# Side operations and stage joins moved by one contraction tile, and weight splits cut, in a two-layer attention and recurrence kernel

## The reference

```python
u = causal_depthwise_conv(cv_a * sigmoid(cv_b), conv_w, conv_b)
u = silu(layernorm(u, conv_ln_g, conv_ln_b))
y_conv = (u @ w_conv_pw) * silu(cv_gate)
x = x + concatenate([y_conv, y_fox, y_mem]) @ w_out
...
q = rms(q, q_g); k = rms(k, k_g)
att = softmax(q @ k.T * scale + bias) @ v * silu(a_z)
hg = rms(hgrn2(g_q, g_f, g_i), o_g) * silu(g_z)
x = x + gate * (concatenate([att, hg]) @ w_out_2)
```

## Time and profile before

| what | value |
|---|---|
| median of 3 runs | 1893.55 us (1892.36 to 1894.06) |
| the profiled execution, its own time | 1892.65 us |
| its span, first to last instruction | 1890.9 us |
| PE busy | 1877.2 us, 99% |
| DVE, ACT, POOL busy | 62%, 42%, 10% |
| chain that ended last | PE 94%, DVE 3%, ACT 2% |

### The profile page before, as it was taken

One profiled execution on the slowest core, in us unless ns is written; L12 is line 12 of the kernel. 1 busy time (PEld: TensorE's weight loads), 2 busy tenths in 40 slices (PEclk: granted clock), 3 DMA queues, 4 the chain that ended last, 5 costly groups with the idle time before them and its releaser, 6 DMA issues.

```text
span 1890.9 us, 25550 instructions
## 1 busy us (share of the span) xinstructions
PE 1877.2 (99%) x8756; PEld 1546.3 (82%) x8756; DVE 1174.7 (62%) x1708; ACT 789.0 (42%) x1155; POOL 187.7 (10%) x193
## 2 busy tenths in 40 slices
PE   9999999999999999999999999999999999999999
PEld 8888888888888877887788888888888888887887
DVE  6665568888888877777745444445555555556332
ACT  6543333333333373224544444444545454554111
POOL 3500000000000002442000000000112121210000
PEclk9999999999999999999999999999999999999999
DMA  7344144544444426775122222221222122123441
GB/s 280 111 156 178 67 158 176 177 177 168 162 164 172 156 89 221 235 244 197 70 92 90 71 88 92 92 92 67 90 82 73 67 89 89 67 89 129 146 147 67
DMA packets 50407, 244.70 MB, mean 129 GB/s; under 512 B 5688, under 2 KB 6968, under 8 KB 29760
## 3 DMA queue, kind: packets, MB, share of 16 engines
q1 hardware_dynamic: 49920, 241.02, 36.0%
q10 hardware_dynamic: 448, 3.17, 0.4%
HBM read 235.75 MB, written 8.41 MB: 129 GB/s over the span
## 4 chain that ended last, share of the span: by engine, by line
PE 94%; DVE 3%; ACT 2%; issue 0%; DVEq 0%; ACTq 0%; another core or an unknown queue 0%
PE ps_p L599 27%; PE ps_p L601 26%; PE ps_p L600 26%; PE ps_s L919 1%; PE ps_o L751 1%; PE ps_t L735 1%; DVE w_lo L1451 1%; PE ps_x L618 1%; DVE act_lo L2012 0%; ACT act_hi L1239 0%; PE ps_s L724 0%; PE ps_s L723 0%; PE ps_s L725 0%; ACT w_hi L1006 0%; PE ps_o L624 0%
## 5 line engine op out<-in xcount | busy, mean ns | idle before, releaser
L599 PE MATMUL ps_p<-act_hi,w_hi 128*128 128x512 f32 x2272 | 910.6, 401 | 3.5 <-DVE act_lo L1855 1.7
L601 PE MATMUL ps_p<-act_hi,w_lo 128*128 128x512 f32 x2272 | 886.7, 390 | 0.0
L600 PE MATMUL ps_p<-act_lo,w_hi 128*128 128x512 f32 x2272 | 885.9, 390 | 0.0
L601 PEld LDWEIGHTS ps_p<-act_hi,w_lo 128*128 128x128 f32 x2272 | 426.5, 188 | 91.6
L599 PEld LDWEIGHTS ps_p<-act_hi,w_hi 128*128 128x128 f32 x2272 | 427.2, 188 | 88.2 <-issue 3.3
L600 PEld LDWEIGHTS ps_p<-act_lo,w_hi 128*128 128x128 f32 x2272 | 427.5, 188 | 80.8 <-issue 1.4
L1006 ACT ACTIVATE w_hi<-raw 128x2048 fp32r<-128x2048 f32 x154 | 294.5, 1912 | 413.7 <-PE ps_p L601 395.2
L1451 DVE TENSOR_TENSOR w_lo<-raw,w_hi 128x2048 fp32r<-128x2048 f32 x153 | 350.8, 2293 | 91.5 <-ACT w_hi L1006 80.1
L1728 DVE CUSTOM_DVE_ANT_0 mkv<-mkv,c_all 128x1024 f32<-128x1024 f32 x96 | 145.0, 1546 | 4.4 <-DVE wk L1493 2.9
L2200 POOL TENSOR_TENSOR hz<-hqk,hd 128x128 f32<-128x128 f32 x56 | 38.8, 693 | 743.7 <-DVEq L2070 692.7
L2187 POOL TENSOR_TENSOR ssq_a<-ssq_a,wk 128x512 f32<-128x512 f32 x15 | 36.3, 2420 | 733.4 <-ACT wk L1259 733.4
(11 more groups left out here) (318 smaller groups left out, 1879.6 us busy)
## 6 DMA issues: line engine op xcount, KB each, us to landing
raw<-wt_dram SPq DMA_DIRECT2D x156, 1024.0 KB, 4.8
mkv<-ada_dram SPq DMA_DIRECT2D x96, 512.0 KB, 4.4
qkv<-xT_dram SPq DMA_DIRECT2D x16, 256.0 KB, 2.8
spill_dram<-Y SPq DMA_DIRECT2D x16, 256.0 KB, 2.2
hqk<-spill_dram SPq DMA_DIRECT2D x16, 256.0 KB, 2.7
out_dram<-wk SPq DMA_DIRECT2D x16, 256.0 KB, 2.0
Y<-xT_dram SPq DMA_DIRECT2D x3, 1024.0 KB, 10.1
mem_raw<-memT_dram SPq DMA_DIRECT2D x4, 512.0 KB, 10.6
```

The costliest lines, as they stand in the source:

```text
L599: mm(o, wh, hi[:, k, 0:n], start=at == 0, stop=False)
L600: mm(o, wh, lo[:, k, 0:n], start=False, stop=False)
L601: last = mm(o, wl, hi[:, k, 0:n], start=False, stop=at == KT - 1)
```

## The change

It moves work on PE, ACT, DVE and SP, and cuts a few instructions in two. No matmul is added or removed.

- Each channel is squared once it is centred. `conv_z(0)` goes ahead of the sum of the squares. PE's two sums go to places 10 and 6.
- `act_hi` and `act_lo` 4 to 7 are rewritten ahead of `ln_silu((2, 3))`. After `pointwise` the low parts lag the multiplications by one tile.
- In the first head of att the query's square goes between the quarters of the third weight tile, the key's square ahead of the fourth weight tile, which is split in halves. PE's sums go to places 2 and 7.
- In hg `chunk_states` goes from place 9 to 10, and `out_sum` from 2 to 3.
- In the last head DVE makes the low parts of tiles 0 and 1 ahead of the turned pairs, and the second weight tile of out2 is split in halves, on the first of which PE starts.
- The last tile's addition and store are cut in halves.

Only the declarations of four semaphores are left out here, beside unchanged lines:

```diff
@@ -567,13 +571,18 @@
                     sp.wait_ge(s_out, 2 * i + j + 1)
+                    if isinstance(i, int) and i + j == 8:
+                        sp.dma_start(out[15][:, 0:S // 2], wk[:, j, 0:S // 2]).then_inc(s_store[j], 16)
+                        sp.wait_ge(s_out, 17)
+                        sp.dma_start(out[15][:, S // 2:S], wk[:, j, S // 2:S]).then_inc(s_store[j], 16)
+                        continue
                     sp.dma_start(out[2 * i + j], wk[:, j, :]).then_inc(s_store[j], 16)
...
             for j in range(2):
-                sp.wait_ge(s_store[j], 16 * 16)
+                sp.wait_ge(s_store[j], 16 * (16 + j))
@@ -581,10 +590,12 @@
             def project(phase, i, j, hi=act_hi, lo=act_lo, n=S, order=range(KT), hooks=None, use=None, used=None,
-                        quartered=False):
+                        quartered=False, halved=False):
                 s = slot(phase, j)
-                if not quartered:
+                if halved:
+                    pe.wait_ge(out_half, 1)
+                elif not quartered:
                     pe.wait_ge(w_split, tile_no(phase, i, j) + 2)
@@ -592,6 +603,8 @@
                         pe.wait_ge(third_split, at // 4 + 1)
+                    elif halved and at == KT // 2:
+                        pe.wait_ge(w_split, tile_no(phase, i, j) + 2)
                     elif use == "y2":
@@ -816,8 +829,8 @@
                 return lambda: side("gate", 0, k, body)
-            project("gate", 0, 0, hooks={9: channel_sum(0)})
-            project("gate", 0, 1, hooks={5: channel_sum(1)})
+            project("gate", 0, 0, hooks={10: channel_sum(0)})
+            project("gate", 0, 1, hooks={6: channel_sum(1)})
             project("gate", 0, 2)
@@ -885,7 +898,7 @@
                     first_pair()
-                    sums, scored = {3: lambda: square_sum(0), 8: lambda: square_sum(1)}, (14, 15)
+                    sums, scored = {2: lambda: square_sum(0), 7: lambda: square_sum(1)}, (14, 15)
                 else:
@@ -970,12 +983,12 @@
-                project("hg", i, 0, hooks=None if isinstance(i, int) and i == 0 else {2: out_sum})
+                project("hg", i, 0, hooks=None if isinstance(i, int) and i == 0 else {3: out_sum})
                 project("hg", i, 1, hooks={15: lambda: side("hg", i, 0, turn_keys)})
...
                                            8: lambda: turn_value("hg", i, 1, hvT[:, :], QT),
-                                           9: chunk_states, 11: turn_pairs, 13: within, 15: across},
+                                           10: chunk_states, 11: turn_pairs, 13: within, 15: across},
                         used=h_used if isinstance(i, int) and i == 7 else None)
@@ -985,7 +998,7 @@
                 project("out2", i, 0, use="y2", hooks={3: last_sum} if first else None)
-                project("out2", i, 1)
+                project("out2", i, 1, halved=first)
             loop(pe, "out2", out2, head=1)
@@ -1212,8 +1225,8 @@
             split("gate", 0, 0)
-            act.wait_ge(ln_ready.sem, ln_ready.at("gate", 0, 1))
             for c in range(NCONV):
+                act.wait_ge(channel_centred, c + 1)
                 fn(qkv[:, c, :], Y[:, c, :], ACT.Square).then_inc(ln_squares, 1)
@@ -1228,20 +1241,24 @@
             split("gate", 0, 2)
-            act.wait_ge(ln_ready.sem, ln_ready.at("gate", 0, 2))
+            act.wait_ge(ln_ready.sem, ln_ready.at("gate", 0, 1))
             ln_silu((0, 1))
...
             split("gate", 0, 3)
-            ln_silu((2, 3))
...
+            def y_hi_used(order_):
+                for k in order_:
+                    act.wait_ge(x_used, k + 1) if k < KT - 1 else act.wait_ge(proj_done, tile_no("out1", 0, 0) + 1)
+                    y_hi([k])
+
             act.wait_ge(heads_done.sem, heads_done.at("fox", 7, 1))
-            for k in range(4, KT):
-                act.wait_ge(x_used, k + 1) if k < KT - 1 else act.wait_ge(proj_done, tile_no("out1", 0, 0) + 1)
-                y_hi([k])
+            y_hi_used(range(4, 8))
+            ln_silu((2, 3))
+            y_hi_used(range(8, KT))
             conv_gate(2)
@@ -1322,17 +1339,21 @@
                         fn(w_hi[:, w, c], raw[:, w, c], ACT.Copy).then_inc(third_hi, 1)
+                        if q == 1:
+                            norm(0)
                     act.wait_ge(third_hi, 4)
                     act.sem_inc(w_hi_done, 1)
-                    norm(0)
-                    split("att", i, 2)
+                    act.wait_ge(side_full.sem, side_full.at("att", i, 1))
+                    norm(1)
+                    w = slot("att", 3)
+                    act.wait_ge(s_raw[w], 16 * (half("att", 0, 3) + 1))
                 else:
...
                 if isinstance(i, int):
-                    norm(1)
+                    fn(w_hi[:, w, 0:D // 2], raw[:, w, 0:D // 2], ACT.Copy).then_inc(fourth_hi, 1)
                     high("att", i, 0, qk2_hi, qkv2)
@@ -1341,6 +1362,8 @@
                 high("att", i, 1, qk2_hi, qkv2)
+                if isinstance(i, int):
+                    fn(w_hi[:, w, D // 2:D], raw[:, w, D // 2:D], ACT.Copy).then_inc(w_hi_done, 1)
                 for t in range(3):
@@ -1796,11 +1819,17 @@
-            def channels_added(c4):
+            def channels_added(c4, squared=False):
+                if squared:
+                    dve.wait_ge(ln_squares, 2)
                 o.step(tt(wk[:, 3, :], c4[:, 0, :], c4[:, 1, :], ALU.add))
                 o.settle()
+                if squared:
+                    dve.wait_ge(ln_squares, 3)
                 o.step(tt(wk[:, 3, :], wk[:, 3, :], c4[:, 2, :], ALU.add))
                 o.settle()
+                if squared:
+                    dve.wait_ge(ln_squares, 4)
                 tt(wk[:, 3, :], wk[:, 3, :], c4[:, 3, :], ALU.add).then_inc(side_in.sem, 1)
@@ -1810,12 +1839,9 @@
             for c in range(NCONV):
-                o.step(tt(Y[:, c, :], Y[:, c, :], ssq_b[:, :], ALU.subtract))
-            o.settle()
-            dve.sem_inc(ln_ready.sem, 1)
-            dve.wait_ge(ln_squares, NCONV)
-            channels_added(qkv)
+                tt(Y[:, c, :], Y[:, c, :], ssq_b[:, :], ALU.subtract).then_inc(channel_centred, 1)
             conv_z(0)
+            channels_added(qkv, squared=True)
             conv_gate(0)
@@ -1842,9 +1868,6 @@
             split("gate", 0, 3)
-            ln_silu((2, 3))
-            o.settle()
-            dve.sem_inc(pw_in.sem, 1)
@@ -1854,7 +1877,11 @@
-            y_lo(range(4, KT))
+            y_lo(range(4, 8))
+            ln_silu((2, 3))
+            o.settle()
+            dve.sem_inc(pw_in.sem, 1)
+            y_lo(range(8, KT))
             conv_gate(2)
@@ -1864,7 +1891,9 @@
                    ALU.mult).then_inc(pw_done.sem, 1)
-                y_lo([m])
+                if m:
+                    y_lo([m - 1])
+            y_lo([NCONV - 1])
             do(dve.memset(ssq_a[:, :], 0.0))
@@ -1964,22 +1993,27 @@
                         split_part(slot("att", 2), slice(q * S, (q + 1) * S), third_hi, q + 1, third_split)
+                        if q == 1:
+                            square_lo("att", i, 0, sq2_hi[:, :], sq2_lo[:, :])
                     dve.wait_ge(third_split, 4)
                     dve.sem_inc(w_split, 1)
-                    square_lo("att", i, 0, sq2_hi[:, :], sq2_lo[:, :])
-                    split("att", i, 2)
+                    square_lo("att", i, 1, sq2_hi[:, :], sq2_lo[:, :])
                 else:
...
                 normed(0, hcol[:, 6, 0:1])
-                square_lo("att", i, 1, sq2_hi[:, :], sq2_lo[:, :])
                 if isinstance(i, int):
+                    split_part(slot("att", 3), slice(0, D // 2), fourth_hi, 1, fourth_split)
                     low("att", i, 0, qk2_lo, qkv2, qk2_hi)
                     o.settle()
-                if not isinstance(i, int):
+                else:
+                    square_lo("att", i, 1, sq2_hi[:, :], sq2_lo[:, :])
                     split("att", i, 2)
                 normed(1, col("k_norm_g_2"))
+                if isinstance(i, int):
+                    dve.wait_ge(fourth_split, 1)
+                    split_part(slot("att", 3), slice(D // 2, D), w_hi_done, tile_no("att", 0, 3) + 2, w_split)
                 dve.wait_ge(s_bias, 16 * i + 16)
@@ -2013,7 +2047,7 @@
-                y2_lo(range(7))
+                y2_lo(range(2, 7))
                 square_lo("hg", i, 0, sq3_hi[:, :], sq3_lo[:, :])
@@ -2026,7 +2060,9 @@
                 y2_lo(range(11, KT))
-                split("out2", 0, 0)
+                w, t = slot("out2", 1), tile_no("out2", 0, 1)
+                split_part(w, slice(0, D // 2), w_hi_done, t + 2, out_half)
+                split_part(w, slice(D // 2, D), w_hi_done, t + 2, w_split)
@@ -2095,6 +2131,8 @@
                 split("hg", i, 3)
+                if isinstance(i, int):
+                    y2_lo(range(2))
                 dve.wait_ge(pair_turned.sem, pair_turned.at("hg", i, 1))
```

(10 more changed lines are left out.)

4 lines of the change are left out of this document (added).

## The result

The changed kernel takes **1881.77 us** (median of 6 runs, 1880.17 to 1882.67), the kernel before beside it 1893.12 (6 runs, 1892.36 to 1894.06): ratio 0.9938, 95% interval 0.9928 to 0.9948. The profiled execution took 1880.25 for a span of 1878.5: 12.4 less than before, where the sum of the prediction was 9.8.

The account below looks back on a forecast made before the run. PE, busy 1877.2 of 1890.9 us, bounds the kernel, so only its waits can be won. Gains of 4.38 + 0.96 + 1.56 + 1.21 + 1.3 + 0.4 = 9.8 us give 1883.8 from 1893.55; range 1882.6 to 1888.0.

Parts of the forecast that it names:

- eight large gaps: PE's waits: gate 0.77, 0.77, 0.49, 0.40; join to out1 1.01; behind pointwise 1.03; att's first head 0.96; out2's second tile 1.07.
- the slacks (0.3 to 0.8): Time to spare before PE waits: 0.3 behind the pointwise product, 0.6 at low part 8, 0.7 and 0.8 elsewhere.
- rival A: Some joins keep a wait because a late semaphore or settling eats the slack: 1885.5 to 1888 us; chance 0.22.
- B: Recurrence gaps are the price of issuing side operations, not data waits, so moving them gains nothing: 1888 to 1891; chance 0.07.
- C: Row sum one tile on becomes the last thing ACT waits for, delaying the weights in seven heads: 1897.6; chance 0.03.
- D: The loops' places moved for head 0 alone; excluded by the order of instructions, with no chance given.
- The time lost at a wait is therefore the idle time in brackets plus 0.16: Rule for all PE waits, measured from the last full-pace product to the waiting one; a shown 0.85 costs 1.01.
- 2.77: Recurrence: gain in us from moving chunk states (1.56) and row sum (1.21) one tile on.
- The join to out2: Last head and start of out2's second tile: earlier low parts and halved weights let PE start sooner, 1.3 us in all.
- The new wait at the products within chunks (L971): Last head: the copy of the turned pairs comes later, so PE's product waits 0.2, eating 0.16 won at the chunk states.
- The half of the weights: Out2's second weight tile: DVE's low part of one half takes 1.15 us, so PE starts near 1722.5, not 1723.85.
- The end: Last tile's addition and store: first half goes out 0.35 earlier, last transfer holds half the bytes; 0.4 us gained.

Follow-up runs that it names:

- experiment 1: The kernel before with only the recurrence's chunk states moved from place 9 to 10 and row sum from 2 to 3: 1888.83 us, ratio 0.9976.
- experiment 4: The changed kernel with one recurrence place moved back: row sum at place 2, 1882.14 us, ratio 0.9942; chunk states at place 9, 1884.23 us, ratio 0.9952.
- experiment 2: The kernel before with only the change's parts in gate and the join to out1: 1888.84 us, ratio 0.9975.

## Why the prediction was right and wrong

**Direction, places and mechanism: right.** All eight large gaps went, since each producer came as early as worked out; none of the slacks (0.3 to 0.8) was eaten, so rival A fell. B fell by experiment 1. C didn't happen: ACT's chain behind the row sum didn't delay anything, and the heads gain alike. D fell with the trace.

**The step that failed** is the first one, "The time lost at a wait is therefore the idle time in brackets plus 0.16", used "everywhere". A wait costs 0.06 to 0.12 more, in the start of the product behind. So the mechanism was right and the price of a wait, a term of every sum, was too small. This size was to be had from the kernel before: in the earlier trace rows L702 stands at 1398.85, and the product behind it, one row further in the same view, at 1399.19. I measured from the product before the wait to the one that waited, and not to the point at which the pace was regained. Per place it is little, but the change removes 23 waits, 15 of them between 0.15 and 0.25 long, where it is a quarter (chunk states) to two thirds (row sum) as much again. In the recurrence 2.77 became 4.48: by experiment 4 the restarts are 1.3 of the 1.7 between, and nearly all of the rest, 0.3, is missing in two other profiles of the same recurrence. In gate and out1 the six restarts are the 0.6 from 4.38 to 4.98, as experiment 2 repeats. In att 0.96 became 1.13: 1.04 at the wait itself, and 0.09 ahead of it that has no explanation. All in all 12.4 - 9.8 = 2.6 is 0.6 + 0.2 + 1.7, and 0.2 at the first matmuls, less 0.1 at the end. Some 2.0 of it is restarts, and some 0.5 is what two executions of the same code differ by.

**The smaller terms.** The join to out2 was right in sum (1.3, measured 1.34), by some luck in its parts. The new wait at the products within chunks (L971) didn't come: the copy of the pairs ran directly behind the two low parts, at 1695.65, which is 0.35 later against DVE's weight split than before, where I had 0.5, and PE's product came at 1696.49 by its place. So the chunk states of head 7 brought their 0.25 and nothing ate it. The wait for low part 11 I had missed altogether: 0.33 before and 0.41 now, so that it took 0.08 away. The second tile brought 1.06. The half of the weights: forecast 1.15, measured 1.22. Here the rule of the Trainium skill that I had set beside it (VectorE: DVE Perf Modes, The TRN2 errata) was the better guide, (1024 + 151) / 0.96 = 1224 ns; the trace has 1219 and 1221 ns. The end: forecast 0.4, measured 0.25. The other rule of the Trainium skill (DMA: Bandwidth & Descriptors, Anatomy of one DMA) gave 0.3. The page states it for a DMA on the gpsimd path, and this store is SP's. By it 256 KB would take 2.6 and 128 KB 2.3; the trace has 2.0 and 1.8, so the step between the sizes is about right here and the fixed part is not. Both figures that I had weighed and not taken, 1.22 and 0.3, were nearer. Together these two errors are 0.2, and they made the forecast too large, while the restarts made it too small.

**What the range lacked.** Its lower end, 1882.6, allowed 1.2 for the end and a neighbour's gap, and no error of the arithmetic that all terms share. A price per wait, repeated 23 times, is such an error. All rivals lay on the side of a smaller gain. The median adds something of its own: 12.4 in the profiled pair, 11.35 between the medians. At a mean clock of 1.0, that of both profiled executions, the runs differ by 12.2 (1892.45, 1880.21), and at 0.999 by 11.7 (1893.51, 1881.83).

## What to carry to other kernels

Count a wait of PE from the last product at full pace to the first one that is at full pace again, not to the one that waited; on the short, frequent waits here the restart is a fifth to two fifths of the price, so moving a side product by a single tile pays more than its gap shows. Before splitting or reordering at a join, look whether an earlier step already clears it: of this change's parts, the silu's order and two early low parts brought nothing that could be measured, while one hole of DVE behind ACT was still to be used. When runs of one kernel fall into two groups, read the granted clock of each, and look for a stretch where PE is idle; here harmless work in it took the slower group away.
